# A 14-slot weight ring and a single-pass fp32r scatter in the expert stage of a two-block transformer kernel

## The reference

```
aff    = sigmoid(x @ router_w)                       # 256 tokens x 16 experts
e_idx  = top 2 experts of the token's best group     # 4 groups of 4
gates  = aff[e_idx] / sum(aff[e_idx])                # zero elsewhere
for each expert e:                                   # in effect
    act  = silu(x @ w_gate[e]) * (x @ w_up[e])       # width 512
    ffn += gates[:, e] * (act @ w_down[e])
x = layer_norm(ALPHA * x + ffn)
```

## Time and profile before

| | |
|---|---|
| median of 3 runs | 1250.47 us (1249.85 to 1250.59) |
| profiled execution, its own time | 1255.39 us |
| span of that execution | 1253.5 us |
| expert stage of layer 0, first raise to last scatter | 586.7 to 812.5 us |
| expert stage of layer 1, first raise to last scatter | 1013.1 to 1239.2 us |

### The profile page before, as it was taken

The page is one execution under the profiler, slowest core; times in us unless marked ns, Lnnn a source line. Parts: engine busy times, 40 slices in busy tenths (PEclk is TensorE's granted clock), DMA queues, the critical chain, the costliest instruction groups (busy, mean ns, idle before and its releaser), DMA issues.

```text
span 1253.5 us, 15635 instructions
## 1 busy us (share of the span) xinstructions
PE 1120.7 (89%) x6095; PEld 762.1 (61%) x6101; DVE 520.8 (42%) x939; ACT 423.9 (34%) x723; POOL 43.7 (3%) x71
## 2 busy tenths in 40 slices
PE   6997987999998998877999999969888599999995
PEld 5896876899997886655334333358777443343332
DVE  5563264666676457545111111164565531111112
ACT  5355433555444435523111111233454211111111
POOL 1200000000000020000000000001100000000000
PEclk9999888999999988797999999978878789999998
DMA  7753042555554330372999999833223659999992
GB/s 275 253 183 115 21 135 68 182 187 201 201 194 174 101 115 34 135 302 79 422 419 421 420 420 421 349 111 105 101 102 128 241 211 420 420 420 421 420 421 116
DMA packets 81842, 296.62 MB, mean 237 GB/s; under 512 B 7156, under 2 KB 40290, under 8 KB 57074
## 3 DMA queue, kind: packets, MB, share of 16 engines
q1 hardware_dynamic: 79168, 289.29, 59.8%
q0 software_dynamic: 1216, 4.27, 1.0%
q10 hardware_dynamic: 1394, 2.18, 0.5%
HBM read 294.68 MB, written 1.05 MB: 236 GB/s over the span
## 4 chain that ended last, share of the span: by engine, by line
PE 64%; issue 23%; DVE 7%; ACT 3%; DMA 2%; POOL 0%; POOLq 0%; SPq 0%; ACTq 0%; DVEq 0%
PE bank L1889 8%; PE bank L1551 8%; PE bank L1552 8%; PE bank L1553 7%; PE bank L1590 5%; PE bank L1591 5%; PE bank L1592 5%; PE bank L1515 4%; PE bank L1898 4%; PE bank L1608 2%; PE bank L1624 2%; PE bank L1920 2%; DMA moe_w<-in_w_up 2%; PE bank L1876 1%; DVE lo L949 1%
## 5 line engine op out<-in xcount | busy, mean ns | idle before, releaser
L949 DVE TENSOR_TENSOR lo<-raw,hi 128x2048 fp32r<-128x2048 f32 (+3 forms) x87 | 186.6, 2162 | 115.7 <-ACT hi L599 115.6
L1172 DVE TENSOR_TENSOR proj<-bank,proj 64x512 f32<-64x512 f32 x32 | 34.6, 1081 | 367.7 <-PE bank L1911 353.5
L599 ACT CAST hi<-raw 128x2048 fp32r<-128x2048 f32 (+3 forms) x87 | 155.1, 1804 | 71.0 <-PE bank L1553 54.5
L1590 PE MATMUL bank<-xs,hi 128*128 128x256 f32 x544 | 153.6, 282 | 4.0 <-DVE lo L949 3.0
L1591 PE MATMUL bank<-xs,hi 128*128 128x256 f32 x544 | 153.0, 281 | 0.0
L1592 PE MATMUL bank<-xs,lo 128*128 128x256 f32 x544 | 152.9, 281 | 0.0
L1551 PE MATMUL bank<-hi,xs 128*128 128x512 f32 (+2 forms) x328 | 134.2, 409 | 10.8 <-DVE gates L1377 5.5
L1552 PE MATMUL bank<-hi,xs 128*128 128x512 f32 (+2 forms) x328 | 128.8, 393 | 0.0
L1553 PE MATMUL bank<-lo,xs 128*128 128x512 f32 (+2 forms) x328 | 128.0, 390 | 0.0
L1889 PE MATMUL bank<-moe_w,xg 128*64 128x512 f32 x240 | 107.9, 592 | 1.9 <-DMA moe_w<-in_w_up 1.9
L1890 PE MATMUL bank<-moe_w,xg 128*64 128x512 f32 x240 | 108.0, 593 | 0.0
(11 more groups left out here) (224 smaller groups left out, 1753.4 us busy)
## 6 DMA issues: line engine op xcount, KB each, us to landing
raw<-in_w_up SPq DMA_DIRECT2D x40, 1024.0 KB, 5.2
moe_w<-in_w_down SPq DMA_DIRECT2D x36, 1024.0 KB, 15.1
moe_w<-in_w_gate SPq DMA_DIRECT2D x30, 1024.0 KB, 13.9
moe_w<-in_w_up SPq DMA_DIRECT2D x30, 1024.0 KB, 16.0
raw<-in_w_in SPq DMA_DIRECT2D x28, 1024.0 KB, 5.4
raw<-in_w_down SPq DMA_DIRECT2D x25, 1024.0 KB, 9.0
q_t<-in_w_gate SPq DMA_DIRECT2D x16, 1024.0 KB, 13.9
k_t<-in_w_up SPq DMA_DIRECT2D x16, 1024.0 KB, 16.0
```

Source lines behind the costliest of these rows:

```text
L599: nc.scalar.copy(hi[:, n % RING, 0:size], raw[:, n % RING, 0:size]).then_inc(S["hi_done"], 1)
L949: tt(lo[:, n % RING, 0:size], raw[:, n % RING, 0:size], hi[:, n % RING, 0:size].bitcast(F32), ALU.subtract).then_inc(S["lo_done"], 1)
L1590: mm(dst, wh[:, k, col], x_hi, start=k == 0, stop=False)
```

## The change

- **Ring.** `MOE_SLOTS` is 14. The two new buffers are `xn` and columns 1024 to 3071 of `proj` (`flat`). Slabs 12 and 13 are issued after the layer's first norm (`ln_done`), slab m from 14 on after slab m - 14 has been used. The buffer counts (`moe_in`) and the wait of the next layer's loads (`last_in_slot`) follow.
- **Scatter.** The map in `slot_to_token` no longer holds the gates but 0 or 1, in fp32r; the gate of each slot is the row's sum (`slot_gate`). The expert's output is multiplied by it and split into a high and a low fp32r part, and `add_out` runs eight fp32r matmuls where it ran four float32 ones.
- **Who does it.** ACT's `turned_copied` copies only the activation's 256 columns; its `out_copied` writes the scaled high part, now into one buffer. DVE gets `mapped` (a row sum and a comparison of 128x256 from bank 3) and `out_split` (the low part, 128x512 from bank 2). The scatter and the next lower wait for `out_split`, the next turn waits for `mapped`.
- **Memory.** `gates` shares its place with the stage's own buffers, and `expert_out`, `slot_to_token`, `act_t` and `hot_gate` are tensors of their own.

```diff
-MOE_SLOTS = 12
+MOE_SLOTS = 14
...
+        moe_slots += [xn[:].rearrange("p a n -> p (a n)"), flat[:, 2 * FFE:2 * FFE + SLAB]]
...
-                    elif 2 * RING <= m < MOE_SLOTS:
+                    elif 2 * RING <= m < 4 * RING:
                         sp.wait_ge(S["slab_used"], b + L_O + 2 + m // 2 - RING)
+                    elif 4 * RING <= m < MOE_SLOTS:
+                        sp.wait_ge(S["ln_done"], 2 * HALVES * layer + HALVES)
                     elif m >= MOE_SLOTS:
                         moe_wait(sp, layer, "moe_used", m - MOE_SLOTS + 1)
...
                 def turned_copied(e):
                     moe_wait(act, layer, "moe_turned", e + 1)
-                    if e >= 2:
-                        moe_wait(act, layer, "moe_scattered", e - 1)
-                    nc.scalar.copy(turned[:, e % 2].rearrange("p v n -> p (v n)"), bank[3][:])\
+                    nc.scalar.copy(act_t[:, e % 2], bank[3][:, 0:SEQ].rearrange("p (c s) -> p c s", s=SLOTS))\
...
                 def out_copied(e):
                     moe_wait(act, layer, "moe_used", first_down(e) + 2)
-                    if e >= 2:
-                        moe_wait(act, layer, "moe_scattered", e - 1)
-                    nc.scalar.copy(expert_out[:, e % 2, :], bank[2][:]).then_inc(S["moe_out_ready"], 1)
+                    moe_wait(act, layer, "moe_map_ready", e + 1)
+                    if e:
+                        moe_wait(act, layer, "moe_scattered", e)
+                    nc.scalar.activation(expert_out[:, 0, :], bank[2][:], ACT.Copy, scale=slot_gate[:, e % 2:e % 2 + 1])\
+                        .then_inc(S["moe_out_high"], 1)
...
+                def mapped(e):
+                    moe_wait(dve, layer, "moe_turned_copied", e + 1)
+                    if e >= 2:
+                        moe_wait(dve, layer, "moe_scattered", e - 1)
+                        moe_wait(dve, layer, "moe_out_high", e - 1)
+                    map_of(e % 2).then_inc(S["moe_map_ready"], 1)
+                def map_of(at):
+                    both = bank[3][:, SEQ:2 * SEQ]
+                    nc.vector.tensor_reduce(slot_gate[:, at:at + 1], both, AX.X, ALU.add)
+                    return nc.vector.tensor_scalar(slot_to_token[:, at, :], both, 0.0, None, ALU.is_gt)
+                def out_low(at):
+                    return nc.vector.scalar_tensor_tensor(out=expert_out[:, 1, :], in0=bank[2][:],
+                                                          scalar=slot_gate[:, at:at + 1],
+                                                          in1=expert_out[:, 0, :].bitcast(F32),
+                                                          op0=ALU.mult, op1=ALU.subtract)
+                def out_split(e):
+                    moe_wait(dve, layer, "moe_out_high", e + 1)
+                    out_low(e % 2).then_inc(S["moe_out_ready"], 1)
...
                 for e in range(EXPERTS):
                     gated(e)
+                    if e:
+                        mapped(e - 1)
                     if e < EXPERTS - 1:
                         gated_slots(e + 1)
                     if e % EPG == EPG - 1 and e // EPG + 2 < EGROUPS:
                         slots_of(e // EPG + 2)
+                    if e:
+                        out_split(e - 1)
+                mapped(EXPERTS - 1)
+                out_split(EXPERTS - 1)
...
                 def add_out(at):
                     for half in range(HALVES):
-                        for c in range(2):
-                            part = slice(SLOTS * c, SLOTS * (c + 1))
-                            ins = mm(acc[half][c][:], slot_to_token[part, at, half * P:(half + 1) * P],
-                                     expert_out[part, at, :], start=False, stop=False)
+                        for split_ in range(2):
+                            for c in range(2):
+                                part = slice(SLOTS * c, SLOTS * (c + 1))
+                                ins = mm(acc[half][c][:], slot_to_token[part, at, half * P:(half + 1) * P],
+                                         expert_out[part, split_, :], start=False, stop=False)
...
-                        moe_wait(pe, layer, "moe_turned_copied", e)
+                        moe_wait(pe, layer, "moe_map_ready", e)
                     turn_hot(e % 2)
```

More of the change, by code:

```diff
@@ L162 @@
               "moe_xg_ready": 4 * EGROUPS, "moe_hot_ready": HALVES * EXPERTS}
-MOE_COUNTS |= {f"moe_in{i}": 16 * (MOE_SLABS // MOE_SLOTS) for i in range(MOE_SLOTS)}
-MOE_COUNTS |= {f"moe_{name}": EXPERTS for name in """silu_done act_gated turned turned_copied out_ready scattered""".split()}
+MOE_COUNTS |= {f"moe_in{i}": 16 * len(range(i, MOE_SLABS, MOE_SLOTS)) for i in range(MOE_SLOTS)}
+MOE_COUNTS |= {f"moe_{name}": EXPERTS for name in """silu_done act_gated turned turned_copied map_ready out_high out_ready scattered""".split()}
 SEMAPHORES += list(MOE_COUNTS)
 SEMAPHORES += """late_places late_in late_equal late_hot late_gathered late_xg late_raised late_silu late_gated
- late_turned late_act late_lowered late_out""".split()
+ late_turned late_act late_map late_lowered late_high late_out""".split()
 def constants():
@@ L247, in build @@
         proj = sb("proj", [P, HALVES, IN2])
-        gates = sb("gates", [P, 2 * DC, SEQ])
         wide_a = sb("wide_a", [P, HALVES * D])
@@ L255, in build @@
         one_hot = sb("one_hot", [P, 2, HALVES, EPG, SLOTS], F32R)
+        slot_gate = sb("slot_gate", [P, 2])
         rounds = sb("rounds", [P, 1], mybir.dt.int32)
@@ L271, in build @@
                 nc.sbuf_tensor("lo", [P, RING, SLAB], F32R) as lo, \
-                nc.sbuf_tensor("act_r", [P, 2 * 2 * 2 * SEQ], F32R) as act_r:
+                nc.sbuf_tensor("act_r", [P, 2 * 2 * 2 * SEQ], F32R) as act_r, \
+                nc.sbuf_tensor("gates", [P, 2 * DC, SEQ], F32) as gates:
             pass
@@ L275, in build @@
         xg = sb("xg", [P, 2, EPG, DC, SLOTS])
+        expert_out = sb("expert_out", [P, 2, 512], F32R)
+        slot_to_token = sb("slot_to_token", [P, 2, SEQ], F32R)
+        act_t = sb("act_t", [P, 2, FFE // P, SLOTS])
+        hot_gate = sb("hot_gate", [P, 2, HALVES, P])
         ident = const[:, C_ID:C_ID + P]
@@ L317, in build @@
         silu_e, act_e = (flat[SLOTS:P, FFE * i:FFE * (i + 1)] for i in range(2))
[L318 to L323, removed]
         place = route[:, 3, :]
@@ L349, in build, with last_in_slot @@
         moe_slots += [moe_w[:, RING * part + i, :] for i in range(RING) for part in range(2)]
+        moe_slots += [xn[:].rearrange("p a n -> p (a n)"), flat[:, 2 * FFE:2 * FFE + SLAB]]
+        def last_in_slot(slot):
+            return max(range(slot, MOE_SLABS, MOE_SLOTS))
         def count(n, j=None, per=0):
@@ L448, in _ @@
                     if layer and i < RING:
-                        moe_wait(sp, layer - 1, "moe_used", MOE_SLABS - MOE_SLOTS + RING + i + 1)
+                        moe_wait(sp, layer - 1, "moe_used", last_in_slot(RING + i) + 1)
                     load(b + L_IN + i, rows_of(w, 2 * i, 2, 0, D))
@@ L925, in late_expert @@
                     act.wait_ge(S["late_turned"], t + 1)
-                    nc.scalar.copy(turned[:, 0].rearrange("p v n -> p (v n)"), bank[3][:]).then_inc(S["late_act"], 1)
+                    nc.scalar.copy(act_t[:, 0], bank[3][:, 0:SEQ].rearrange("p (c s) -> p c s", s=SLOTS))\
+                        .then_inc(S["late_act"], 1)
+                    act.wait_ge(S["late_map"], t + 1)
                     act.wait_ge(S["late_lowered"], t + 1)
-                    nc.scalar.copy(expert_out[:, 0, :], bank[2][:]).then_inc(S["late_out"], 1)
+                    nc.scalar.activation(expert_out[:, 0, :], bank[2][:], ACT.Copy, scale=slot_gate[:, 0:1])\
+                        .then_inc(S["late_high"], 1)
                 earlier = late_experts(act, more, earlier, late_expert)
@@ L1208, in late_expert @@
                     tt(act_out(act_e), by_slab(bank[1][SLOTS:P, :]), by_slab(silu_e), ALU.mult).then_inc(S["late_gated"], 1)
+                    dve.wait_ge(S["late_act"], t + 1)
+                    map_of(0).then_inc(S["late_map"], 1)
+                    dve.wait_ge(S["late_map"], t + 1)
+                    dve.wait_ge(S["late_high"], t + 1)
+                    out_low(0).then_inc(S["late_out"], 1)
                 return late_experts(dve, more, earlier, late_expert)
@@ L1948, in scatter_expert @@
                 def scatter_expert(e):
-                    moe_wait(pe, layer, "moe_turned_copied", e + 1)
+                    moe_wait(pe, layer, "moe_map_ready", e + 1)
                     moe_wait(pe, layer, "moe_out_ready", e + 1)
```

## The result

The changed kernel takes 1239.99 us (median of 4 runs, 1238.46 to 1242.63), where the kernel before took 1250.53 us beside it (4 runs, 1249.85 to 1253.58): a ratio of 0.9912, 95% interval 0.9892 to 0.9932. The difference is 10.5 us; 12.3 was forecast. The profiled execution took 1238.46 us, its span 1236.7.

A forecast was written before the change was run, and what follows sets the result against it. In the expert stages PE and DMA were taken to limit within 1 us, DMA slower by 0.7 us per expert. Layer 0 -6.1 and layer 1 -6.2 make -12.3: 1250.47 - 12.3 = 1238.2 us, range 1234 to 1247.

The forecast's parts named there:

- Both limits, 1 us apart: Expert stages: PE 14.23 us an expert, DMA 14.96 with 12 slabs in hand; the two limits meet within 1 us.
- Two slots, 2 x 2.49 = 4.98 us: Expert stage: slabs 12 and 13 go out near 563, so the last gate/up pair lands 4.98 us earlier.
- The scatter, 1.00 us: PE's scatter per expert falls from 1.92 to 1.00 us, saving 0.92; 7.6 us of the saving become waiting for slabs.
- ACT's scaled copy at nothing: ACT copies half as much of bank 3 and scales where it copied: no cost.
- `out_split` 0.75, shown only at the end: DVE's low part is hidden in the steady loop; before scatter 14 it adds 0.75 us with its hand-over.
- The sum: Terms after the last pair's landing added: layer 0 -6.1 us, layer 1 -6.2, together -12.3.
- The base: Forecast put against the median, 1250.47 us, not the profiled 1255.39; work between the stages only moved, 3 us either side.
- (a): Rival: TensorE's clock falls to 0.50 in the new waits of the last experts; 1241 to 1248 us, chance 0.11.
- (b): Rival: scatter's weight loads wait for their own row group, 1.68 us a scatter; 1243.4 us, chance 0.06.
- (c): Rival: scatter's matmul pairs don't overlap, 1.84 us, PE stays the limit; 1248.3 us, chance 0.07 given with (e).
- (d): Rival: no overlap and exposed weight loads, 3.4 us a scatter; slower, 1295.4 us, chance 0.04.
- (e): Rival: the two slots bring nothing, only the tail is gained; 1248.1 us, chance 0.07 given with (c).

The follow-up runs named there:

- the two halves: 14-slot ring alone on the kernel before: ratio 0.9980, stages -2.3 us; changed kernel held to 12 slabs in flight: ratio 0.9964, stages -0.6 us.
- the kernels of the table: The changed kernel and its follow-up variants, each run beside the kernel before; medians from 1226.07 us (16 slots, earlier last lower) to 1267.84 (8 slabs in flight).
- the line of six points: Changed kernel with 8, 10, 12, 13, 14 and 16 slabs in flight: stages +19.7, +9.7, -0.6, -5.6, -10.4, -20.2 us against the kernel before.

## Why the prediction was right, step by step

- **Both limits, 1 us apart.** Shown by the two halves: -2.3 and -0.6 alone, -10.4 together.
- **Two slots, 2 x 2.49 = 4.98 us.** In layer 0 the last pair landed 198.46 us after SP's issue into the first freed slot, where 198.1 was forecast and before had 203.1: -4.66. PE starts on it 787.23 - 588.64 = 198.59 after that issue. The term is 0.3 us too large, in layer 1 about 0.5; where those tenths go stays open. The two slabs issued near 563: 561.20 and 561.58, in an execution that is 2.2 us early there.
- **The scatter, 1.00 us.** It took 1.12, so the saving is 0.80 and not 0.92, and the period with a gather 13.44 and not 13.3. In the source view the eight weight loads have a median of 185 ns and the matmuls of 393 ns; the chain's 1.12 us is four pairs about 0.25 us apart and a start-up. The waits for slabs follow: with 13 x 0.80 = 10.4 in place of 12.0, and 4.66 in place of 4.98, the 7.6 us become 6.4; the list of waits has 5.5. The timeline shows where the rest is, here at the last wait:

```profile
785.28 0.59 PE L1936 MATMUL bank<-raw,xg 128*64 128x512 f32 x1
...
787.23 0.61 PE L1936 MATMUL bank<-moe_w,xg 128*64 128x512 f32 x1 [1.32 <-DMA moe_w<-in_w_up]
```

  Without a wait these matmuls start 0.43 us apart, so this one is 787.23 - 785.28 - 0.43 = 1.52 us late, and the list counts 1.32. Five times 0.2 more makes the 5.5 into 6.5.
- **ACT's scaled copy at nothing.** It was 0.69 us where the plain copy took 0.58, 0.1 more, and lies on the path of the tail. That term was missing.
- **`out_split` 0.75, shown only at the end.** 0.76 in the chain, with its hand-over 0.79. Scatter 14 starts 797.87 - 796.23 = 1.64 us after lower 14 ends, where 1.5 was forecast and before had 0.78. In both layers PE's scatter waited for DVE just twice, at the last two scatters, 2.6 us in all:

```profile
PE bank L1968 <- DVE expert_out L1199: 2.6, 2, 1.7
```

- **The sum.** Layer 0: the pair -4.67, scatter 13 -0.80, the way to scatter 14 longer by 0.89 and the scatter shorter by 0.80, and nothing from lower 15 on (10.57 before, 10.56 now, so the last scatter's saving was indeed lost): -5.4, where -6.1 stood. Layer 1: to lower 15 -5.16, behind it +0.11 where -0.17 stood: -5.05, where -6.2 stood. The forecast of -12.3 is thus 1.9 too much, about 0.8 of it the slots' term, 0.5 to 0.6 the scatter and the rest ACT's copy and the hand-overs.
- **The base.** Between the stages the profiled executions differ in the clock's spells. Windows from the end of layer 0's stage to the first freed slot of layer 1, first of the kernel before and then of the changed one:

```profile
810.30:1016.79 206.49, 163.41 (x796) 134.75 (x800) 117.37 (x284) 83.95 (x183) 14.95 (x29) 0.83 0.33 120
```

```profile
803.28:1005.00 201.72, 157.75 (x798) 130.45 (x800) 117.75 (x285) 83.81 (x183) 14.97 (x29) 0.85 0.37 134
```

  The same work took 4.8 us less in the second, at a mean clock of 0.85 in place of 0.83. Most of that is an execution's own: in the second profile of the changed kernel the same stretch took 204.53 us at 0.83. The kernel before has one profile only, so a small part for the change isn't ruled out by it; the medians less the stages, 800.8 us before and 800.7 after, leave it none. That the forecast was put against the median and not against this execution was therefore right: the spans alone differ by 16.8 us. That the base then held within 0.1 us is luck in part, as the same remainder goes from 798.0 to 804.7 us over the kernels of the table.

**The rivals.** (a) The clock fell in the waits: no, it is 1.00 in all windows over the waits, with PE at 79% of its time and, with 8 slabs in flight, at 86% over 40 us. Why it fell in the earlier trace rows, behind a stretch in which PE was busy 73% of the time, and not here, no run tells. (b) Weight loads wait for their own row group, 1.68 us a scatter: it takes 1.12 in either order. The Trainium skill's rule ("TensorE: Matmul & The Clock Gate", Part 3, The mechanism) that a load runs ahead only into other rows is therefore not what this trace shows for loads of 64 rows either; by it the sum would have been -7.0. (c) No overlap of the pairs, and (d) slower: out by the same 1.12 us. (e) The slots bring nothing: out by the line of six points.

## What to carry to other kernels

When two engines, or an engine and the DMA, run at nearly the same pace, each improvement tried by itself measures as next to nothing; look for the wait that would appear, and try the two together before dropping either. A ring in front of a steady stream is worth its head start: every buffer filled while the stream would idle takes one transfer off the end, up to where the consumer is the limit. And the path behind the last item is to be read apart from the steady loop: work that is hidden fourteen times is paid for at the last two.

## What the runs showed of the hardware that I had not expected

The value of a slab in flight is a straight line from 8 to 16 of them, 4.8 to 5.1 us for each over two layers in the stages, with 420 GB/s throughout; more requests in the queue were served neither faster nor slower. And the exchange of the scatter's inner loops, which puts two matmuls of the same 64 rows one behind the other, left its time at 1.12 to 1.13 us, where it was expected to cost some 0.4 us.
